# Attention of the prompt: probabilities turned in two halves of 64 query rows, and the weighted values of two head pairs done in one piece

## The reference

```python
# for each block of 128 query rows, each head, each of the branches CMP, SLC, WIN (NSA) and FOX
l = einsum(q, k) * HEAD_DIM ** -0.5 + bias          # scores, HEAD_DIM = 64
p = softmax(masked l)                               # f32, over the keys that the block may see
o = einsum(p, v)                                    # weighted values
o_nsa = g0 * o_cmp + g1 * o_slc + g2 * o_win        # the three NSA branches, gated, are summed
```

## Time and profile before

| | |
|---|---|
| three runs, median | 2426.54 us |
| profiled execution, span | 2428.4 us |
| TensorE busy in it | 2369.9 us (98%) |
| stretch of the prompt's attention | 361.5 to 745.0 us |
| in this stretch: TensorE, VectorE, ScalarE, GpSimd busy | 359.48, 270.13, 238.55, 187.05 us |
| granted TensorE clock in this stretch | 1.00 |

### The profile page before, as it was taken

The page is one execution under the profiler, slowest core; times in us unless marked ns, Lnnn a source line. Parts: engine busy times, 40 slices in busy tenths (PEclk is TensorE's granted clock), DMA queues, the critical chain, the costliest instruction groups (busy, mean ns, idle before and its releaser), DMA issues.

```text
span 2428.4 us, 30908 instructions
## 1 busy us (share of the span) xinstructions
PE 2369.9 (98%) x10983; PEld 1532.6 (63%) x10983; DVE 1236.0 (51%) x3115; ACT 547.6 (23%) x1328; POOL 834.1 (34%) x874
## 2 busy tenths in 40 slices
PE   8999999999998999999999999999999999999999
PEld 4544665555556777688886458888888874443343
DVE  4876716776773444522322794433334324229765
ACT  0001016666663333111111221111011110001131
POOL 0000004554454000475753453334333227203531
PEclk9999999999999999999999999999999999999999
DMA  5423830021018887632325301111111115543201
GB/s 185 106 82 86 273 113 20 1 81 59 1 57 226 234 232 199 209 87 78 87 73 156 83 31 53 36 36 53 35 46 42 36 48 202 175 143 135 84 18 57
DMA packets 185956, 240.28 MB, mean 99 GB/s; under 512 B 53436, under 2 KB 128834, under 8 KB 184266
## 3 DMA queue, kind: packets, MB, share of 16 engines
q1 hardware_dynamic: 181018, 218.99, 29.4%
q10 hardware_dynamic: 1168, 9.58, 1.3%
q0 software_dynamic: 3616, 9.73, 1.2%
HBM read 216.18 MB, written 37.99 MB: 105 GB/s over the span
## 4 chain that ended last, share of the span: by engine, by line
PE 56%; DVE 2%; ACT 1%; issue 0%; DVEq 0%; ACTq 0%
PE ps L2218 36%; PE ps L2382 11%; PE ps L2271 5%; PE ps L2439 2%; PE ps L2369 1%; DVE xT L153 1%; PE ps L2447 1%; ACT xT L2492 0%; PE ps L2275 0%; DVE arena L2970 0%; ACT arena L2589 0%; DVE stats L2644 0%; PE ps L2314 0%; DVE queries L2973 0%; DVE arena L1364 0%
## 5 line engine op out<-in xcount | busy, mean ns | idle before, releaser
L2218 PE MATMUL ps<-xT,arena 128*128 128x272 f32 x1920 | 472.7, 393 | 1.3 <-DVE arena L1375 1.3
L2218 PEld LDWEIGHTS ps<-xT,arena 128*128 128x128 f32 x1920 | 363.9, 190 | 77.0 <-DVE arena L1375 1.7
L2218 PE MATMUL ps<-queries,arena 128*128 128x272 f32 x1312 | 332.6, 393 | 1.8 <-DVE queries L2785 1.0
L2218 PEld LDWEIGHTS ps<-queries,arena 128*128 128x128 f32 x1312 | 249.6, 190 | 54.1 <-DVE queries L2785 1.4
L236 PE MATMUL ps<-arena,xT 128*128 128x512 f32 (+1 forms) x512 | 198.0, 549 | 2.1 <-DMA arena<-in_w_in 1.3
L1008 POOL TENSOR_SCALAR arena<-arena,gates 128x55 f32<-128x55 f32 (+15 forms) x192 | 123.2, 652 | 176.6 <-DVE arena L907 176.4
L943 ACT ACTIVATE arena<-arena 128x640 f32<-128x640 f32 (+15 forms) x256 | 164.7, 643 | 69.0 <-DVE arena L899 49.1
L236 PEld LDWEIGHTS ps<-arena,xT 128*128 128x128 f32 x512 | 97.7, 191 | 102.0 <-issue 93.0
L2218 PE MATMUL ps<-arena 128*128 128x272 f32 x576 | 148.6, 394 | 0.0
L798 PE MATMUL ps<-ident,arena 128*128 128x128 f32 (+4 forms) x880 | 137.8, 284 | 11.0 <-POOL arena L1008 5.2
L786 PE MATMUL ps<-arena,queries 64*128 64x512 f32 (+11 forms) x704 | 128.8, 465 | 14.2 <-DVE arena L899 11.4
(11 more groups left out here) (345 smaller groups left out, 3275.8 us busy)
## 6 DMA issues: line engine op xcount, KB each, us to landing
arena<-in_cache_fox_kv SPq DMA_DIRECT2D x72, 256.0 KB, 4.3
arena<-in_w_ffn_down SPq DMA_DIRECT2D x68, 256.0 KB, 3.3
arena<-in_w_in SPq DMA_DIRECT2D x16, 1024.0 KB, 5.3
xT<-in_w_ffn_down SPq DMA_DIRECT2D x64, 256.0 KB, 3.9
xT<-in_cache_fox_kv SPq DMA_DIRECT2D x56, 256.0 KB, 6.2
arena<-in_cache_nsa_kv SPq DMA_DIRECT2D x64, 192.0 KB, 7.8
arena<-in_w_ffn_up SPq DMA_DIRECT2D x11, 1024.0 KB, 5.4
arena<-in_w_ffn_gate SPq DMA_DIRECT2D x11, 1024.0 KB
```

The costliest lines, as they stand in the source:

```text
L2218: mm = pe.matmul(ps[:, first + BANK_OF[z], 0:PIECE], weight[:, j, :], moving[:, j, :], start=(j == 0 and z in (1, 6, 5, 7)), stop=(j == kk ...
```

## The change

A turn no longer goes head by head. Each transposition takes 64 query rows (`rows`) of one head and one key tile, with a 64x64 part of the identity; the lower 64 rows go to the one bank, the upper 64 to the other, and the four transpositions of a key tile (two heads, two halves of rows) are issued with the halves of rows in turn. Both banks, both scalings and both copies are waited for ahead of the whole turn, and both banks are complete at its end. ScalarE's copy now takes query rows 0 to 63 of both heads, VectorE's rows 64 to 127. The weighted values of a pair with j = 1 are done in one piece, both parts one after the other, after the second chunk's turn of the next pair. In the diff the hunk at line 912 is VectorE's copy, the one at 949 ScalarE's.

```diff
@@ -789,14 +789,21 @@
             def turn(p, c):
                 t0, m = p.chunks[c]
-                for half, turned, saved in ((0, turned_a, saved_b), (1, turned_b, saved_a)):
-                    if c == 0:
-                        pe.wait_ge(normed, 2 * p.n + half + 1)
-                    if TURNED_BEFORE[p.n] + c + half >= 2:
-                        pe.wait_ge(saved, TURNED_BEFORE[p.n] + c + half - 1)
-                    for x, (kt, s, w) in enumerate(p.tiles[t0:t0 + m]):
-                        mm = pe.transpose(ps[0:w, turn_bank(p, c, half), x * P:(x + 1) * P], probs_of(p, half, s, w), keep.ident[:])
-                    mm.then_inc(turned, 1)
+                if c == 0:
+                    pe.wait_ge(normed, 2 * p.n + 2)
+                before = TURNED_BEFORE[p.n] + c
+                if before >= 2:
+                    pe.wait_ge(saved_b, before - 1)
+                if before >= 1:
+                    pe.wait_ge(saved_a, before)
+                for x, (kt, s, w) in enumerate(p.tiles[t0:t0 + m]):
+                    for half in range(2):
+                        for r in range(2):
+                            rows = slice(r * HD, (r + 1) * HD)
+                            mm = pe.transpose(ps[0:w, turn_bank(p, c, r), (2 * x + half) * HD:(2 * x + half + 1) * HD],
+                                              probs_of(p, half, s, w)[rows], keep.ident[rows, rows])
+                            if half == 1 and x == m - 1:
+                                mm.then_inc((turned_a, turned_b)[r], 1)
...
-            def values_beside(n):
-                for part in (1, 0):
-                    q = n - 1 - part
-                    if 0 <= q < NPAIR and PAIRS[q].j == 1:
+            def values_behind(n):
+                q = n - 1
+                if 0 <= q < NPAIR and PAIRS[q].j == 1:
+                    for part in range(2):
                         weighted_values(PAIRS[q], part)
...
                 if p.n + AHEAD < NPAIR:
                     scores(PAIRS[p.n + AHEAD])
-                values_beside(p.n)
                 if len(p.chunks) > 1:
                     turn(p, 1)
-            values_beside(NPAIR)
-            values_beside(NPAIR + 1)
+                values_behind(p.n)
+            values_behind(NPAIR)
@@ -912,8 +918,8 @@
-                nc.vector.tensor_copy(turned_of(p)[0:w, t0:t0 + m, 1, p.j, :],
-                                      ps[0:w, turn_bank(p, c, 1), 0:m * P].rearrange("p (t q) -> p t q", t=m)).then_inc(saved_b, 1)
+                nc.vector.tensor_copy(turned_of(p)[0:w, t0:t0 + m, :, p.j, HD:P],
+                                      ps[0:w, turn_bank(p, c, 1), 0:m * P].rearrange("p (t h q) -> p t h q", t=m, h=2)).then_inc(saved_b, 1)
@@ -949,8 +955,8 @@
-                nc.scalar.copy(turned_of(p)[0:w, t0:t0 + m, 0, p.j, :],
-                               ps[0:w, turn_bank(p, c, 0), 0:m * P].rearrange("p (t q) -> p t q", t=m)).then_inc(saved_a, 1)
+                nc.scalar.copy(turned_of(p)[0:w, t0:t0 + m, :, p.j, 0:HD],
+                               ps[0:w, turn_bank(p, c, 0), 0:m * P].rearrange("p (t h q) -> p t h q", t=m, h=2)).then_inc(saved_a, 1)
```

## The result

The changed kernel took 2474.9 us in the median of four runs (2468.3 to 2476.5), the kernel before 2426.8 beside it: 1.0177 times as long, 95% interval 1.0160 to 1.0195. That is 39 to 47 us slower; 2422 was forecast, and the range ended at 2446. The profiled execution of after has a span of 2466.5 us, 38.1 above that of before, and that difference is what the traces can explain. The other three executions took 5 to 8 us more, at a mean granted clock of 0.973 to 0.974 against its 0.976.

The account below looks back on a forecast made before the run. TensorE was taken to bound the prompt's attention, with logits and scaling chains nearly as long behind it. Of 45 + 22 us gross, the walk left 1.8 per turn of heads, about 4 us off: 2422 us, range 2402 to 2446.

Parts of the forecast that it names:

- the walk through the new order: One wide tile stepped through by old durations: f1's scores 0.11 us later, next w0 0.48 earlier; other tiles walked alike.
- the sum: Prompt's attention, net gain on the path: two turns of heads give 3.6 us, taken as 4 us off.
- waits grow by some 50 us: Expected sign: TensorE's waits for GpSimd and VectorE's logits together grow this much, its busy time falling by about as much.
- Values: Weighted values: same products in one piece, twice as many in one step, with the next turn and scores queued behind.
- the 1.8 per turn of heads: Prompt's attention: us gained per turn of heads; narrow tiles give 0.5 to 1 each, a wide tile's f1 or s1 takes one back.
- Turns: TensorE's transposes: 96 us before, 51 after at 0.058 per pair, 45 less; bounds 51 and 96.
- Rival C: Turns: row halves take turns at 0.109 us a step instead of overlapping; 2446 us, chance 0.11.
- Copies: Copies of turns out of PSUM: same elements in runs of 64, old time kept; bounds nothing and 0.1 us each.
- Changes of shape: TensorE's array switches: turns and scores now share 64x128, saving 22 us at most, from below nothing.
- The bare copies: Turns waiting for ScalarE's copy of the turn before: 0.85 us for four tiles, 0.52 for one, 16 us together.
- Rival B: Bare copies decide: 23 waits of 0.52 to 0.85 us come whole on the path, +16 us, 2442 us; chance 0.11.
- Rival A: TensorE's saving comes through: 40 us less the 16 us of bare copies, 2403 us; chance 0.23.

Follow-up runs that it names:

- e10: e5 with 198 extra products ahead of turns and 104 ahead of scores, where its trace shows TensorE waiting; 2424.7 us, 0.9974 to 0.9993 of before.
- e11: e2 with 36 extra products of 128 rows ahead of turns and 103 ahead of scores, filling its waits; 2445.6 us, 1.0056 to 1.0090 of before.
- e9: Changed kernel with 278 extra products ahead of turns and 116 ahead of scores, filling TensorE's waits; 2443.7 us, 1.0055 to 1.0088 of before.
- e2: Kernel before with only the values changed: old turns, values in one piece behind the second turn; 2453.2 us, 1.0067 to 1.0122 of before.
- e5: Changed kernel's new turns, but values in two parts, behind the second chunk's turn; 2431.2 us, 0.9984 to 1.0015 of before.
- e8: e4 with the values in two parts at their old place; 2437.6 us, 1.0021 to 1.0049 of before.
- e4: Changed kernel, all lower-row transposes before all upper, only the second half waiting for ScalarE's copy; 2477.2 us, 1.0166 to 1.0204 of before.
- e1: Changed kernel's new turns only, values in two parts at their old place; 2433.7 us, 1.0004 to 1.0024 of before.

## Why the prediction was wrong

**The step that failed: the durations in the walk through the new order.** Every term was taken from rows at a granted clock of 1.00, the walk added them up, and the sum let TensorE wait more at no other price: the clock stood in it at nothing, without a reason. A second step failed with it, the price of the values in one piece (below). The prediction itself foresaw "waits grow by some 50 us"; it didn't ask what TensorE's clock does with them. The three terms, if they add up, from the profiled stretches: new turns at full clock -4.0 (e10 against before), values in one piece at full clock +15.4 (e11), and 38.2 - 11.4 = 26.8 that neither has. e9 bounds this rest from the other side: 24.4 us of after's loss went away when nothing changed but the filling of waits, and 20.5 us of low time were left. So some 25 of the 38 us are the clock, at 0.28 us per us of lower level (24.4 for 88.7); e2 to e11 gives 0.32, e5 to e10 0.17, though e10's extra products cost time of their own (33.15 us for tile 7, 30.96 in e5, both at full clock). What in the waits makes the clock fall is not settled: the long stretch of tile 7 in after has 13 us without work in 51.2 and stays at 1.00 until it falls at 559.0, and the narrow one from 402.0 has 3 of 20.4 without work and stays at 0.50; work itself lasts longer there, so the rows don't tell which waits count.

The Trainium skill's page "TensorE: Matmul & The Clock Gate", section "A second HAM failure mode: psum-queue depth-cycling", describes a kernel in which short idle times between groups of products, as it cycles through PSUM banks, make the clock swing between its two levels. This case's traces agree as far as the swing goes: turns go through three banks, the waits of after are at most 3.0 us long, and its clock was 0.87. But before goes through the same three banks at 1.00, so the banks alone don't do it. It would have been the rival that the prediction lacked.

**Values: right in kind, mis-sized.** "Behind them on TensorE's queue stand the next turn and then scores(n + 4), for which VectorE waits" is what e11 shows; the price was taken from f1 of one wide tile (0.11 later) and the other tiles "walked alike". Measured at full clock, one piece costs 0.5 to 3.1 us in each of fourteen stretches (e11 against before, from the start of one w0's logits to the next, where before had no low clock), and 15.4 in the whole stretch.

**The walk** was near for half a tile. From the scores of w0 it had w1 after 6.43, f0 after 9.39, f1 after 15.17 us; measured 6.62, 9.69, 15.48. Then it lost the wait of 2.50 behind f1, and could not see the 3.4 us of low clock from 559.0 on: the next w0 at 32.22 by the walk, at 34.03 in the trace. Neither the 0.48 that it saw there nor the 1.8 per turn of heads came. That the -4 of the sum agrees with e10's -4.0 is an accident: the sum held the lump, e10 doesn't.

**Turns: right.** 0.52 us for sixteen was forecast, 0.52 measured. An estimate by the Trainium skill's page "TensorE: Matmul & The Clock Gate", section "LDWEIGHTS (loading the stationary operand)", is 0.86 us, eight steps of 107 ns. This case's traces don't agree: 0.52 here, and steps of 0.060 in e8, where one half's transposes follow each other. The measurement decides against the rule for this load. Rival C is dead in after. **Copies: right**, 684 and 581 ns for four key tiles (VectorE, ScalarE), 686 and 577 before. **Changes of shape: right in kind**, "issue" before scores in 92 places for 154, and no gap between a turn and its scores; but that wait fell from 32.7 to 27.8 us only (17.0 in e10, at full clock), and no run shows the 22 us.

**The bare copies: about the size, another weight.** Between two turns with nothing else, the end of the first (540.96 + 0.52) and the start of the next (542.41) lie 0.93 apart; 0.85 was forecast. ScalarE's copy ends at 542.27, and the turn starts 0.14 behind it, where 0.06 was taken. By the profile's rows these waits grew by 17 us, from 7 to 24.0, where 16 were forecast. What they cost is not settled: e4 takes most of them away and gains nothing, but its turns are slower. Rival B had the sign and not the size; if the three terms add up, the clock and the values make up the loss without its cause.

**Rival A** asked that turns and changes of shape come through on the path; at full clock 4 of 67 us did, and e10's extra products hide some more (2.2 in tile 7's first turn of heads, 33.15 against 30.96).

## What to carry to other kernels

Where an engine with a clock of two levels stands at 98% busy, taking work off it can gain nothing (e1: 42 us less, and no faster): ask what fills the waits that open, and price the half clock as a rival of its own. Work that covers a wait for another engine is worth its place; put together in one piece ahead of that wait, it both delays the other engine and uncovers the wait. To tell a lost clock from a bad order, fill the waits with useless products and look whether the time falls, and set the times of several executions of one kernel beside their clocks.

## What the runs showed of the hardware

- 394 useless products made the kernel 1% faster (e9 against after), as the low time went from 109.2 to 20.5 us.
- Sixteen transposes of 64 rows that alternate between the two halves of the array start within 0.50 us (after); all on one half and then all on the other, within 0.80 (e8).
- Ten executions of one kernel (e5) lay between 2426.2 us, at a mean clock of 0.992, and 2442.1, at 0.984.
